# Root-mean-square norms: the inverse root by logarithm and exponential on the scalar engine, in place of an addition and a reciprocal on the vector engine around a root

## The chip, the cores and the metric

One core of one Trainium2 chip runs a whole two-block network in a single launch. The metric is the device time of that launch in microseconds (us). Five engines work side by side, each through its own list of instructions in order, and meet only at semaphores: TensorE (PE), VectorE (DVE), ScalarE (ACT), GpSimd (POOL) and SyncE (SP, which here only issues transfers).

## The reference: what is computed

A first block (adaptive norm, a mixer of four gated-delta-rule heads and four retention heads, a SwiGLU layer) and a second block (adaptive norm, windowed attention, a state-space scan and grid attention side by side, a merge, a convolutional feed-forward layer, a final norm), on 1024 latent tokens and 256 context tokens of 1024 features, all in fp32. What the change touches are the inverse roots in its norms:

```python
def rms_norm(x, g):
    y = xf * lax.rsqrt(jnp.mean(xf * xf, axis=-1, keepdims=True) + NORM_EPS)
def head_group_norm(t, g):
    return (t - mu) * lax.rsqrt(var + NORM_EPS) * g.astype(jnp.float32)
def l2_normalize(t):
    return t * lax.rsqrt(jnp.sum(t * t, axis=-1, keepdims=True) + NORM_EPS)
```

They are taken of the block's inputs (over 1024 features), of eight q and k heads of the delta rule (over 128), of its four outputs and of four retention outputs (over 128), of the state-space output (over 1024), of the q and k heads of grid attention (over 64), and of the residual stream (four times, over 1024).

## The kernel before, in words

The program is a row of stages, each with one function per engine (`gp_pe`, `gp_act`, `gp_dve`, `gp_pool` and so on). The order of each engine's instructions is the order in which these functions write them; there is no scheduler. Tiles are features (128 partitions) by tokens (up to 512 columns), and `LAT` is the two latent ranges of 512 tokens, `ALL` those and the context's 256. A `Ring` hands out buffers in turn; who takes one waits until the last user of that buffer has given it back. PSUM is eight banks of 128 x 512, mostly one ring, so a bank that is given back late can hold up PE.

Nearly every norm has one pattern. ACT squares the tile (`sq`), PE multiplies the squares by a matrix of ones, which leaves in a bank the sum over features, repeated over all partitions. Then DVE reads the bank and forms mean + epsilon in SBUF (`tensor_scalar`) and gives the bank back, ACT takes the square root in place (`AF.Sqrt`), and DVE inverts it in place (`reciprocal`). Only then the tile is multiplied by it, on DVE or on POOL.

The places, with the tiles' names in the profile:

- First stage (`a_*`, class `Rms`): `rstd`, three ranges. The three means and the three reciprocals stand between DVE's nine small steps of the modulation product `ad1` (`row` copies and `mod` additions), at the places that the tables `DUE` and `INV` name.
- Projection stage of the delta rule (`gp_*`): a first `softplus` for the decays (`tmp`), then twelve blocks m of q, k and v in the order k4 to k7, q0 to q3, v8 to v11. For a block PE multiplies three (or two) column ranges of h by w_in (`hT,wslot`), ACT copies them out (`raw`) and scales the first tap of a 5-tap convolution (`acc<-raw,par`), DVE adds the other four taps (`acc<-raw,par,acc`), ACT applies SiLU (`kT<-acc` or `qT<-acc`) and squares (`raw<-kT`), and PE sums (`raw,cst`). The inverse roots of a block (`rst`) come in DVE's list ahead of the taps of the next block, and POOL multiplies (`kT<-kT,rst`). PE's sums of block m-1 stand between the second and the last column range of block m. From the fifth block on ACT also copies the products of k by k out of the banks (`Wd`, `ktok`, `sq<-bank`).
- Gates of the delta rule and of retention (class `Gate`): `rgate`, four heads of two ranges each, while PE multiplies h by the gate's weights, and DVE also reduces tiles of the modulation matrix (`at1a`), with one small product of PE behind each.
- Projection of grid attention (class `AttGroup`, groups at20 and at21, `proj_*`): seven items of k and q, and in step j PE multiplies item j, sums the squares of item j-1, and rotates item j-2 (`at20qa`). `at20qc` holds the inverse root. For q DVE also multiplies by 1/8. Windowed attention (at10, at11) has the same functions without a norm.
- The residual stream's norms (class `SumSq`, tile `rcs`, 128 x 8) and the start of the second block (`fn_*`), and the state-space output (`ssr`).

ACT's functions lie in table sets, and an instruction ACT_TABLE_LOAD brings in another set. Before, none is written by hand; each stands ahead of the first activation that needs it.

Of the kernel before, what the change touches and what calls it, by code (L numbers as in the profile page):

```python
# [8 lines left out]
EPS = 1e-6  # L9
# [3 lines left out]
def const_tables():  # L13
# [19 lines left out]
        ("offB", ((i // 32) < (j // 32)).astype(f)),  # L33
    ]
# [62 lines left out]
def build(nc, io, out):  # L97
# [81 lines left out]
    class Eng:  # L179
# [124 lines left out]
    ident, ones = C("ident"), C("ones")  # L304
    hs = [slice(x * 128, (x + 1) * 128) for x in range(4)]
# [141 lines left out]
    class Rms:  # L447
# [48 lines left out]
        def mean_dve(self, e, n0, n):  # L496
            r = self.rstd[:, n0:n0 + n]
            e.wait_ge(*self.st.pe.after(self.nm, "sum", n0, self.nk - 1))
            e.tensor_scalar(r, self.banks[self.nm, n0][:, 0:n], self.inv, EPS, OP.mult, OP.add).then_inc(self.st.dve(self.nm, "ms", n0), 1)
            self.banks.give((self.nm, n0), self.st.dve.now())  # L500

        def inverse_dve(self, e, n0, n):
            r = self.rstd[:, n0:n0 + n]
            e.wait_ge(*self.st.act.after(self.nm, "rt", n0))
            e.reciprocal(r, r).then_inc(self.st.dve(self.nm, "rs", n0), 1)

        def dve(self, e):
            for n0, n in self.rngs:
                self.mean_dve(e, n0, n)
            for n0, n in self.rngs:  # L510
                self.inverse_dve(e, n0, n)
# [29 lines left out]
    def softplus(st, nm, x, y, tmp):  # L541
# [58 lines left out]
    DUE, INV = {0: 0, 2: 1, 5: 2}, {5: 0, 6: 1, 7: 2}  # L600
    nm1 = NormMod(n1, "h", xav, h1, ALL, [1, 0, 0], ad1.mv, 1, 0, "norm_mix_g", rstd, gs1, lambda n0: n1.dve.after("x", "rs", n0))
# [24 lines left out]
    def a_act(e):  # L626
# [5 lines left out]
        rms1.roots(e)  # L632
# [358 lines left out]
    def gp_act(e):  # L991
# [77 lines left out]
    def gp_dve(e):  # L1069
# [11 lines left out]
        def norm(m):  # L1081
            dst, rng = gp_dst(m)
            rst = rsts.take("rst", m)
            for ev in rsts.freed("rst", m):
                e.wait_ge(*ev)
# [3171 lines left out]
```

## Time and profile before

| what | value |
|---|---|
| three timed runs | 4667.87, 4677.79 and 4679.56 us, median 4677.79 |
| profiled execution, first to last instruction (span) | 4674.6 us |
| time of the profiled execution apart from its span | not given; the span is 3.2 us under the median of the runs |
| PE busy | 91% of the span |
| DVE busy | 51% |
| ACT busy | 33% |
| POOL busy | 19% |
| DVE, ACT and PE instructions | 3800, 2988 and 18566 |

The table is of averages over stages that differ: in the long matrix products PE has no gap, in others it waits for a chain through ACT and DVE. What an instruction less is worth shows only at the waits of the stage in which it stands. The rows for that are in the section below.

### The profile page before, as it was taken

To read this page: it belongs to the slowest core of one execution; us is meant where nothing else is said; L and a number is where in the kernel's file an instruction comes from. 1 tells how busy PE (TensorE), PEld (TensorE's weight loads), DVE (VectorE), ACT (ScalarE), POOL (GpSimd) and SP (SyncE) were. 2 spreads that over 40 slices of the span, in tenths; PEclk is the share of its full clock that TensorE was granted. 3 is DMA by queue.
4 is the path that set the end of the run, shared out by engine and by line. 5 is a ranking of instruction groups with operands and counts; after the bars stand their busy time and mean duration, and the time that the engine had idled before them with its cause. 6 is when DMAs were issued, how large, how long until landed. Compare 5 with 4: busy or idle time off the path is not lost.

```text
span 4674.6 us, 46418 instructions
## 1 busy us (share of the span) xinstructions
PE 4273.7 (91%) x18566; PEld 3110.9 (67%) x18566; DVE 2382.1 (51%) x3800; ACT 1548.5 (33%) x2988; POOL 905.8 (19%) x695
## 2 busy tenths in 40 slices
PE   7896789999999999997979999899888998999997
PEld 3455754767788888655557866565665677888886
DVE  2768864162556663336262327574657744333334
ACT  3465641122211111333233215352544633222222
POOL 2112224131344441007061000001000021000001
PEclk9898899999999999897979999999999999999999
DMA  5112243112333342211111210111000031111111
GB/s 194 41 61 86 73 133 107 34 52 81 86 113 113 113 115 59 88 58 62 39 61 49 82 44 19 37 57 56 17 23 19 19 117 37 54 45 54 43 39 63
DMA packets 257800, 308.90 MB, mean 66 GB/s; under 512 B 19072, under 2 KB 209936, under 8 KB 256304
## 3 DMA queue, kind: packets, MB, share of 16 engines
q1 hardware_dynamic: 238096, 227.15, 15.8%
q0 software_dynamic: 17408, 75.64, 5.2%
q8 instruction: 146, 2.39, 0.2%
q10 hardware_dynamic: 2080, 3.15, 0.2%
q14 instruction: 70, 0.57, 0.0%
HBM read 271.61 MB, written 34.28 MB: 65 GB/s over the span
## 4 chain that ended last, share of the span: by engine, by line
PE 61%; DVE 10%; ACT 5%; issue 1%; POOL 1%; DMA 0%; POOLq 0%; DVEq 0%; ACTq 0%
PE bank L193 60%; PE bank L196 2%; DVE Mx L205 1%; ACT Mx L202 1%; ACT at21P L202 1%; ACT at20P L202 1%; POOL sq L205 1%; DVE at20sm L223 1%; DVE at21sm L223 1%; DVE x L211 0%; DVE wfl L205 0%; DVE at21Pl L205 0%; DVE at11sm L223 0%; DVE at20Pl L205 0%; DVE at10sm L223 0%
## 5 line engine op out<-in xcount | busy, mean ns | idle before, releaser
L193 PE MATMUL bank<-h,wslot 128*128 128x512 f32 (+2 forms) x1616 | 686.4, 563 | 13.7 <-ACT h L202 3.6
L193 PE MATMUL bank<-hT,wslot 128*128 128x512 f32 (+3 forms) x1136 | 462.7, 564 | 15.9 <-DVE hT L211 7.3
L193 PEld LDWEIGHTS bank<-h,wslot 128*128 128x128 f32 (+1 forms) x1616 | 291.3, 191 | 242.3 <-issue 224.9
L193 PEld LDWEIGHTS bank<-hT,wslot 128*128 128x128 f32 (+1 forms) x1136 | 212.2, 189 | 241.6 <-issue 235.3
L193 PE MATMUL bank<-ffn1h,wfh 128*128 128x512 f32 x704 | 279.9, 398 | 11.8 <-DVE ffn1l L211 10.9
L211 DVE SCALAR_TENSOR_TENSOR x<-bank,mod,x 128x512 f32<-128x512 f32 x224 | 164.3, 746 | 245.4 <-PE bank L193 245.0
L193 PE MATMUL bank<-ffn2h,wgh 128*128 128x512 f32 x704 | 276.3, 392 | 10.0 <-DVE ffn2l L211 9.5
L193 PE MATMUL bank<-ffn1l,wfh 128*128 128x512 f32 x704 | 275.1, 391 | 0.0
L193 PE MATMUL bank<-ffn2l,wgh 128*128 128x512 f32 x704 | 274.7, 390 | 0.0
L193 PE MATMUL bank<-ffn1h,wfl 128*128 128x512 f32 x704 | 274.6, 390 | 0.0
L193 PE MATMUL bank<-ffn2h,wgl 128*128 128x512 f32 x704 | 274.5, 390 | 0.0
L205 DVE TENSOR_TENSOR wfl<-wslot,wfh 128x1024 fp32r<-128x1024 f32 (+2 forms) x92 | 150.3, 1634 | 148.1 <-ACT wfh L202 148.1
L205 POOL TENSOR_TENSOR ffn2al<-ffn2ga,ffn2ah 128x512 fp32r<-128x512 f32 x44 | 57.7, 1312 | 654.9 <-ACT ffn2ah L202 654.9
L226 DVE TENSOR_REDUCE at2a<-ffn1t 128x128 f32<-128x1024 f32 x72 | 143.1, 1988 | 47.8 <-POOL ffn1t L205 47.8
L205 POOL TENSOR_TENSOR sq<-sq 128x512 f32<-128x512 f32 (+1 forms) x77 | 95.0, 1233 | 361.0 <-ACT sq L202 356.8
L193 PEld LDWEIGHTS bank<-ffn1h,wfh 128*128 128x128 f32 x704 | 132.5, 188 | 44.7 <-DVE ffn1l L211 10.6
L193 PEld LDWEIGHTS bank<-ffn2h,wgh 128*128 128x128 f32 x704 | 132.5, 188 | 43.5 <-DVE ffn2l L211 10.6
L211 DVE SCALAR_TENSOR_TENSOR ffn2ga<-ffn2gw,par,ffn2ga 128x1024 f32<-128x1024 f32 x44 | 56.5, 1285 | 199.4 <-ACT ffn2ga L202 198.6
L193 PEld LDWEIGHTS bank<-ffn1h,wfl 128*128 128x128 f32 x704 | 132.6, 188 | 28.0
L193 PEld LDWEIGHTS bank<-ffn2h,wgl 128*128 128x128 f32 x704 | 132.6, 188 | 27.7
L193 PEld LDWEIGHTS bank<-ffn2l,wgh 128*128 128x128 f32 x704 | 132.6, 188 | 26.8
L193 PEld LDWEIGHTS bank<-ffn1l,wfh 128*128 128x128 f32 x704 | 132.8, 189 | 25.5
(573 smaller groups left out, 9512.8 us busy)
## 6 DMA issues: line engine op xcount, KB each, us to landing
wslot<-in_w_in SPq DMA_DIRECT2D x40, 1024.0 KB, 5.7
ffn1t<-in_w_mod POOLq DMA_DIRECT2D x64, 512.0 KB, 4.8
wslot<-in_w_ffn_in SPq DMA_DIRECT2D x44, 512.0 KB, 5.3
Mx<-acsT SPq DMA_DIRECT2D x32, 512.0 KB, 4.9
at1w<-in_ada_w POOLq DMA_DIRECT2D x24, 512.0 KB, 4.7
wslot<-in_ffn_w_gate SPq DMA_DIRECT2D x22, 512.0 KB, 4.0
wslot<-in_ffn_w_up SPq DMA_DIRECT2D x22, 512.0 KB, 5.3
wslot<-in_w_ffn_out SPq DMA_DIRECT2D x20, 512.0 KB, 5.4
```

The lines of the kernel that those rows point to most:

```text
L193: return Counted() if counting[0] else self.q.matmul(o, l, r, start=start, stop=stop)
L196: return Counted() if counting[0] else self.q.transpose(o, i, ident)
L202: return Counted() if counting[0] else self.q.activation(o, i, f, **k)
L205: return Counted() if counting[0] else self.q.tensor_tensor(o, a, b, op)
L211: return Counted() if counting[0] else self.q.scalar_tensor_tensor(o, a, s, b, op0, op1)
L223: return Counted() if counting[0] else self.q.reduce_max(o, a, AX.X)
L226: return Counted() if counting[0] else self.q.reduce_sum(o, a, AX.X)
```

## The change

Every such pattern but those of softmax is rewritten: 1/sqrt(v) is formed as exp(-0.5 ln v). ACT reads the sum from the bank itself (`AF.Ln`, with the 1/n as its scale and epsilon as its bias, a 128 x 1 pointer into three new constant columns), gives the bank back, and applies `AF.Exp` with scale -0.5 in place. DVE's `tensor_scalar` and `reciprocal` are gone. In the q blocks, where the factor 1/8 or 1/sqrt(128) belongs to the root, it goes into scale and epsilon (64 or 128 times each), so DVE's multiplication by 1/8 goes too. Whoever used the inverse root now waits for ACT. Table loads are written by hand: `ln_exp_table` brings the set that has both functions, and `exp_table` brings the exponential's own set at the end of each attention projection. `softplus`, which takes an exponential and then a logarithm, starts with the first of these.

```diff
+        ("eps", np.broadcast_to(np.array([EPS, 64 * EPS, 128 * EPS], f), (128, 3))),
...
+        def ln_exp_table(self):
+            if not counting[0]:
+                self.q.preload_act_table_set("natural_log_exp_and_others")
+
+        def exp_table(self):
+            if not counting[0]:
+                self.q.preload_act_table(AF.Exp)
...
-        def roots(self, e):
-            for n0, n in self.rngs:
-                e.wait_ge(*self.st.dve.after(self.nm, "ms", n0))
-                r = self.rstd[:, n0:n0 + n]
-                e.activation(r, r, AF.Sqrt).then_inc(self.st.act(self.nm, "rt", n0), 1)
+        def root(self, e, n0, n):
+            r = self.rstd[:, n0:n0 + n]
+            e.wait_ge(*self.st.pe.after(self.nm, "sum", n0, self.nk - 1))
+            e.activation(r, self.banks[self.nm, n0][:, 0:n], AF.Ln, scale=self.inv, bias=eps(1)).then_inc(self.st.act(self.nm, "ln", n0), 1)
+            self.banks.give((self.nm, n0), self.st.act.now())
+            e.wait_ge(*self.st.act.now())
+            e.activation(r, r, AF.Exp, scale=-0.5).then_inc(self.st.act(self.nm, "rs", n0), 1)
...
         def act(e):
+            e.ln_exp_table()
             e.wait_ge(*d.after(nm, "abs"))
             e.activation(ex, ex, AF.Exp, scale=-1.0).then_inc(a(nm, "exp"), 1)
...
     def a_dve(e):
         consts(e)
         for g in range(9):
-            if g in DUE:
-                rms1.mean_dve(e, *ALL[DUE[g]])
             ad1.dve(e, g)
-            if g in INV:
-                rms1.inverse_dve(e, *ALL[INV[g]])
...
         def norm(m):
-            rst = rsts["rst", m]
-            for n0, n in gp_dst(m)[1]:
-                e.wait_ge(*gp.dve.after("ss", m, n0))
-                e.activation(rst[:, n0:n0 + n], rst[:, n0:n0 + n], AF.Sqrt, scale=1.0 / QS ** 2 if m < 4 else 1.0).then_inc(gp.act("rt", m, n0), 1)
+            dst, rng = gp_dst(m)
+            rst = rsts.take("rst", m)
+            for ev in rsts.freed("rst", m):
+                e.wait_ge(*ev)
+            x = 128 if m < 4 else 1
+            e.ln_exp_table()
+            for n0, n in rng:
+                e.wait_ge(*gp.pe.after("norm", m, n0))
+                e.activation(rst[:, n0:n0 + n], bk_p["norm", m, n0][:, 0:n], AF.Ln, scale=float(x), bias=eps(x)).then_inc(gp.act("ln", m, n0), 1)
+                bk_p.give(("norm", m, n0), gp.act.now())
+            for n0, n in rng:
+                e.wait_ge(*gp.act.after("ln", m, n0))
+                e.activation(rst[:, n0:n0 + n], rst[:, n0:n0 + n], AF.Exp, scale=-0.5).then_inc(gp.act("rs", m, n0), 1)
...
-            for n0, n in rng:
-                e.wait_ge(*gp.pe.after("norm", m, n0))
-                e.tensor_scalar(rst[:, n0:n0 + n], bk_p["norm", m, n0][:, 0:n], EPS, None, OP.add).then_inc(gp.dve("ss", m, n0), 1)
-                bk_p.give(("norm", m, n0), gp.dve.now())
-            for n0, n in rng:
-                e.wait_ge(*gp.act.after("rt", m, n0))
-                e.reciprocal(rst[:, n0:n0 + n], rst[:, n0:n0 + n]).then_inc(gp.dve("rs", m, n0), 1)
...
                 if tn:
                     r = self.rsr[tn][:, 0:tn[3]]
-                    e.wait_ge(*st.dve.after("ms", *tn))
-                    e.activation(r, r, AF.Sqrt).then_inc(st.act("rt", *tn), 1)
+                    isq = tn[0] == "q"
+                    e.wait_ge(*st.pe.after("nm", *tn))
+                    e.activation(r, bk["nm", *tn][:, 0:tn[3]], AF.Ln, scale=1.0 if isq else 1.0 / 64, bias=eps(64 if isq else 1)).then_inc(st.act("ln", *tn), 1)
+                    bk.give(("nm", *tn), st.act.now())
+                    e.wait_ge(*st.act.now())
+                    e.activation(r, r, AF.Exp, scale=-0.5).then_inc(st.act("rs", *tn), 1)
...
             for gr in self.groups:
                 barrier(e, *gr.before)
                 gr.proj_act(e)
+                e.exp_table()
                 barrier(e, gr.sj)
                 gr.act(e)
```

`Gate`, `SumSq`, `fn_*` and the state-space output are changed in the same way.

Where the lists move, first on ACT, at the delta rule's `softplus` (`tmp`, `negA`, `bet`) and the copies `raw` of block k4 behind it. Before:

```order
L202 ACTIVATE ab<-bank 128x160
L202 ACT_TABLE_LOAD
L202 ACTIVATE tmp<-tmp 128x80
L202 ACT_TABLE_LOAD
L202 ACTIVATE tmp<-tmp 128x80
L202 ACT_TABLE_LOAD
L202 ACTIVATE negA<-par 128x80
L202 ACT_TABLE_LOAD
L202 ACTIVATE bet<-ab 128x80
L202 ACTIVATE raw<-bank 128x256
```

and of the change, at the same place:

```order
L203 ACTIVATE ab<-bank 128x160
L207 ACT_TABLE_LOAD
L203 ACTIVATE tmp<-tmp 128x80 x2
L203 ACTIVATE negA<-par 128x80
L203 ACT_TABLE_LOAD
L203 ACTIVATE bet<-ab 128x80
L203 ACTIVATE raw<-bank 128x256
```

Two of four table loads are gone there. The other two `softplus` calls change in the same way, and over the whole program ACT's list goes from 72 loads to 67.

Second, DVE's list in the projection stage, from the taps of k4 to those of k5 (the part for `rst` is that of the norm of k4). Before:

```order
L208 TENSOR_SCALAR nbet<-bet 128x80
L211 SCALAR_TENSOR_TENSOR acc<-raw,par,acc 128x1284 x4
L208 TENSOR_SCALAR rst<-bank 128x256
L208 TENSOR_SCALAR rst<-bank 128x512 x2
L217 RECIPROCAL rst<-rst 128x256
L217 RECIPROCAL rst<-rst 128x512 x2
```

and of the change:

```order
L217 TENSOR_SCALAR nbet<-bet 128x80
L220 SCALAR_TENSOR_TENSOR acc<-raw,par,acc 128x1284 x16
L223 COPY Gc<-bank 128x10x4 x2
L214 TENSOR_TENSOR kdf<-bank,Gc 128x80
L214 TENSOR_TENSOR bG<-bG,nbet 128x80
```

The norm of each block is gone from between the taps of two blocks, so that the taps of four blocks follow one another. The taps of the next block no longer have a norm of the last one ahead of them.

Third, ACT's list for the norm of k4, which stands ahead of the last `raw` copy and the first tap of k5. Before:

```order
L202 ACTIVATE raw<-bank 128x256
L202 ACTIVATE raw<-bank 128x512
L202 ACT_TABLE_LOAD
L202 ACTIVATE rst<-rst 128x256
L202 ACTIVATE rst<-rst 128x512 x2
L202 ACTIVATE raw<-bank 128x512
L202 ACTIVATE acc<-raw,par 128x1284
```

and of the change:

```order
L203 ACTIVATE raw<-bank 128x256
L203 ACTIVATE raw<-bank 128x512
L207 ACT_TABLE_LOAD
L203 ACTIVATE rst<-bank,cst 128x256
L203 ACTIVATE rst<-bank,cst 128x512 x2
L203 ACTIVATE rst<-rst 128x256
L203 ACTIVATE rst<-rst 128x512 x2
L203 ACTIVATE raw<-bank 128x512
L203 ACTIVATE acc<-raw,par 128x1284
```

One activation for each range is added there, and the number of loads is the same. PE's and POOL's lists do not change.

## Rows read from the trace of the kernel before

**Rows 1.** The page's first part: busy time of each engine.

```profile
PE 4273.7 (91%) x18566; PEld 3110.9 (67%) x18566; DVE 2382.1 (51%) x3800; ACT 1548.5 (33%) x2988; POOL 905.8 (19%) x695
```

**Rows 2.** Windows, all engines: the projection stage, and twenty us within it.

```profile
105.00:375.00 270.00, 226.70 (x677) 118.80 (x675) 192.18 (x184) 138.31 (x229) 36.30 (x27) 0.92 0.15 47
285.00:305.00 20.00, 19.73 (x62) 11.22 (x63) 10.51 (x6) 17.62 (x37) 3.79 (x3) 0.91 0.30 93
```

**Rows 3.** Groups by line and form: count, busy us, mean ns, idle before.

```profile
L217 DVE RECIPROCAL rst<-rst 128x512 f32<-128x512 f32 x16 | 52.3, 3309 | 14.2 <-ACT rst L202 14.0
L217 DVE RECIPROCAL at20qc<-at20qc 128x512 f32<-128x512 f32 x6 | 20.1, 3349 | 0.1
...
L202 ACT ACT_TABLE_LOAD x72 | 92.4, 1283 | 32.5 <-DMA par<-in_par 8.2 <-DVE gsc L211 5.3 <-PE bank L193 4.2
L202 ACT ACTIVATE at20P<-bank,at20sm 128x512 f32<-128x512 f32 x64 | 43.4, 683 | 14.3 <-DVE at20sm L208 14.3
```

**Rows 4.** Timeline of DVE, end of the first stage: start, us.

```profile
63.04 3.34 DVE L217 RECIPROCAL rstd<-rstd 128x512 f32<-128x512 f32 x1
66.30 0.10 DVE L205 TENSOR_TENSOR mod<-bank,par 128x4 f32<-128x4 f32 x1
```

**Rows 5.** Timeline of ACT, softplus of the delta rule.

```profile
110.13 1.28 ACT L202 ACT_TABLE_LOAD   x1
111.42 0.27 ACT L202 ACTIVATE tmp<-tmp 128x80 f32<-128x80 f32 x1
...
114.76 1.34 ACT L202 ACTIVATE raw<-bank 128x256 f32<-128x256 f32 x3
```

**Rows 6.** PE's waits from 104 to 375 us: in total, times, longest.

```profile
PE bank L193 <- ACT raw L202: 18.8, 8, 7.1
PE bank L196 <- ACT acc L202: 3.7, 1, 3.7
PE bank L196 <- DVE ktok L214: 3.3, 1, 3.3
PE bank L196 <- ACT kT L202: 2.3, 1, 2.3
```

**Rows 7.** Timeline of PE, projection stage: start, us, and in brackets idle before.

```profile
125.76 4.63 PE L193 MATMUL bank<-raw,cst 128*128 128x256 f32 x6 [7.05 <-ACT raw L202]
...
211.55 3.75 PE L193 MATMUL bank<-raw,cst 128*128 128x512 f32 x4 [3.85 <-ACT raw L202]
...
285.27 3.48 PE L193 MATMUL bank<-raw,cst 128*128 128x512 f32 x4 [2.94 <-ACT raw L202]
...
312.69 8.73 PE L193 MATMUL bank<-hT,wslot 128*128 128x512 f32 x16
...
352.73 7.03 PE L193 MATMUL bank<-hT,wslot 128*128 128x512 f32 x16
```

**Rows 8.** Timelines of DVE, ACT and POOL, blocks k4 and k6.

```profile
117.53 6.33 DVE L211 SCALAR_TENSOR_TENSOR acc<-raw,par,acc 128x1284 f32<-128x1284 f32 x4 [2.44 <-ACT acc L202]
160.17 7.12 DVE L211 SCALAR_TENSOR_TENSOR acc<-raw,par,acc 128x1284 f32<-128x1284 f32 x4
...
157.99 0.60 ACT L202 ACTIVATE raw<-bank 128x512 f32<-128x512 f32 x1 [4.90 <-PE bank L193]
...
160.34 2.42 POOL L205 TENSOR_TENSOR kT<-kT,rst 128x512 f32<-128x512 f32 x1 [1.94 <-DVE rst L217]
```

**Rows 9.** PE's waits from 600 to 740 us: gate and retention projection.

```profile
PE bank L193 <- ACT rr L202: 2.1, 1, 2.1
PE bank L193 <- DVE mod L205: 1.9, 2, 0.9
...
PE bank L193 <- DVE at1a L226: 1.4, 1, 1.4
```

**Rows 10.** PE's waits from 3197 to 3290 us: grid attention's projection.

```profile
PE bank L193 <- DVE at20qa L211: 2.4, 3, 1.4
```

**Rows 11.** Timeline of ACT, start of grid attention.

```profile
3277.56 1.28 ACT L202 ACT_TABLE_LOAD   x1 [4.13 <-DVE at20sm L208]
```

More of the change, by code:

```diff
@@ L494, in pool @@
                     sqr.give((self.nm, n0, k - 1), self.st.pool.now())
[L496 to L511, printed above, removed]
     class NormMod:
@@ L631, in a_act @@
         rms1.squares(e, [x.after("in") for x in xa_in])
-        rms1.roots(e)
+        e.ln_exp_table()
+        for n0, n in ALL:
+            rms1.root(e, n0, n)
         nm1.act(e)
@@ L1114, in gp_dve @@
         for i, m, rngs in QKV:
[L1115 to L1117 removed]
+            if i > 8:
                 v_tokens(m - 1)
@@ L1599, in root @@
             def root(x):
+                rst = self.rsts.take("r", x)
+                for ev in self.rsts.freed("r", x):
+                    e.wait_ge(*ev)
+                e.ln_exp_table()
                 for n0, n in LAT:
-                    r = self.rsts["r", x][:, n0:n0 + n]
-                    e.wait_ge(*st.dve.after("ms", x, n0))
-                    e.activation(r, r, AF.Sqrt).then_inc(st.act("rt", x, n0), 1)
+                    e.wait_ge(*st.pe.after("norm", x, n0))
+                    e.activation(rst[:, n0:n0 + n], self.bk["norm", x, n0][:, 0:n], AF.Ln, scale=1.0 / 128, bias=eps(1)).then_inc(st.act("ln", x, n0), 1)
+                    self.bk.give(("norm", x, n0), st.act.now())
+                for n0, n in LAT:
+                    e.wait_ge(*st.act.after("ln", x, n0))
+                    e.activation(rst[:, n0:n0 + n], rst[:, n0:n0 + n], AF.Exp, scale=-0.5).then_inc(st.act("rs", x, n0), 1)
             root(0)
@@ L1646, in norm @@
             def norm(x):
-                rst = self.rsts.take("r", x)
-                for ev in self.rsts.freed("r", x):
-                    e.wait_ge(*ev)
-                for n0, n in LAT:
-                    e.wait_ge(*st.pe.after("norm", x, n0))
-                    e.tensor_scalar(rst[:, n0:n0 + n], self.bk["norm", x, n0][:, 0:n], 1.0 / 128, EPS, OP.mult, OP.add).then_inc(st.dve("ms", x, n0), 1)
-                    self.bk.give(("norm", x, n0), st.dve.now())
+                rst = self.rsts["r", x]
                 for n0, n in LAT:
                     r, a = rst[:, n0:n0 + n], self.y[:, self.at(x, n0, n)]
-                    e.wait_ge(*st.act.after("rt", x, n0))
-                    e.reciprocal(r, r).then_inc(st.dve("rs", x, n0), 1)
-                    e.wait_ge(*st.dve.now())
+                    e.wait_ge(*st.act.after("rs", x, n0))
                     e.stt(a, a, P(self.gname), r, OP.mult, OP.mult).then_inc(st.dve("n", x, n0), 1)
@@ L2622, in fn_act, with root @@
         barrier(e, ffn1.st, at2.st)
-        e.wait_ge(*d.after("v1"))
-        e.activation(rn1[:, :], rn1[:, :], AF.Sqrt).then_inc(a("s1"), 1)
+        e.wait_ge(*ffn1.ss.st.pe.end())
+        def root(r, s, key):
+            e.activation(r, s, AF.Ln, scale=1.0 / D, bias=eps(1)).then_inc(a("ln", key), 1)
+            e.wait_ge(*a.now())
+            e.activation(r, r, AF.Exp, scale=-0.5).then_inc(a(key), 1)
+        e.ln_exp_table()
+        root(rn1[:, :], bank[6][:, 0:16].rearrange("p (c w) -> p c w", w=2)[:, :, 0], "r1")
         e.wait_ge(*cx_in.after(1))
@@ L2633, in fn_act @@
         squares(range(2))
-        e.wait_ge(*d.after("v2"))
-        e.activation(rn2[:, :], rn2[:, :], AF.Sqrt).then_inc(a("s2"), 1)
+        e.wait_ge(*d.after("q2"))
+        root(rn2[:, :], rn2[:, :], "r2")
         squares(range(2, 8))
-        e.wait_ge(*d.after("vc"))
-        e.activation(rcc, rcc, AF.Sqrt).then_inc(a("sc"), 1)
+        e.wait_ge(*fn.pe.after("cs"))
+        root(rcc, bank[4][:, 0:2], "rc")
         for n0, n in ALL[1:] + ALL[:1]:
@@ L3315, in sz_act @@
             if (kind, m) == ("g", 2):
-                rms_y.roots(e)
+                e.ln_exp_table()
+                for n0, n in LAT:
+                    rms_y.root(e, n0, n)
         for t in range(18, 24):
@@ L3621, in proj_act @@
             st, bk = self.sj, self.bk
+            if not self.win:
+                e.ln_exp_table()
             for j in range(len(self.items) + 2):
```

72 lines of the change are left out of this document (18 added, 54 removed).

## The prediction

> **What bounds the kernel now.** I read the page's busy times first: PE is busy 91% of the span, DVE 51%, ACT 33% [rows 1]. So PE's own instructions set most of the time, and this change touches none of them. All that it can win is time in which PE stands still for a chain through ACT and DVE, and the work taken from DVE is no measure of it. That work is large: a reciprocal of a 128x512 tile takes 3.3 us [rows 3], and forty-eight of that size go, some 160 us. The share of those that PE waits for must be read stage by stage, so next came the windows: in the projection stage of the delta rule PE works 226.7 of 270 us at a mean clock of 0.92, and DVE 192.2 [rows 2]. That is the stage where DVE could be late. Then PE's waits of each stage that holds a norm: 28.1 us in the projection stage [rows 6], 5.4 in the gate and behind it [rows 9], 2.4 in each of two grid-attention projections [rows 10]. In the retention gate and around the state-space output PE has no wait on these tiles, and I count nothing there though eight and two reciprocals go. The timelines then showed, for each wait, whether a reciprocal or a table load lies on the chain that ends it.
>
> **What the pieces cost.** A mean and a reciprocal leave DVE, a root on ACT becomes two activations. The trace has no Ln and no Exp on these tiles. The nearest row is an activation that reads a 128x512 bank with a pointer as bias, 683 ns [rows 3], and I take that for both at most. A chain over DVE, ACT and DVE, 3.3 us of it the reciprocal, becomes at most 1.4 us on ACT alone. A table load takes 1.28 us, and the next activation starts 0.01 us after its end [rows 5]. The list has five fewer of them.
>
> A page speaks otherwise: by the Trainium skill, "ScalarE: Activation LUTs", section "What ACT_TABLE_LOAD costs", a switch costs about 2.66 us, the load and a drain of 1.38. By that page each load off the path would be worth twice what the rows say. The trace shows no such drain, so the sum goes by 1.28, and the other is a rival below.
>
> **The change part by part.**
>
> *First stage.* DVE's last reciprocal runs from 63.04 us, and the last `mod` addition, on which all of the norm's multiplications wait, has to stand behind it until 66.30 [rows 4]. PE's part of that addition is done some 0.5 us after the reciprocal starts (an estimate from the length of PE's four small products there). Gain 2.8 us, at least 0 and at most 3.3. The banks of the first two sums are now given back by ACT behind its squares, a little later for PE in mid-stage, ahead of weights that it waits for anyway: nothing.
>
> *Softplus of the delta rule.* Two loads go from a chain that has no slack: the `raw` copies start right behind it at 114.76 [rows 5], DVE's taps behind those, and PE waits 7.05 us for the squares at the end [rows 7]. Gain 2.5.
>
> *Blocks k4 to v8.* Here the chain per block is: PE's last range, ACT's `raw` copy and first tap, DVE's four taps, SiLU, square, PE's sum. The reciprocals of the last block lie ahead of the taps. In k6 the taps start at 160.17, only 0.2 us after ACT's first tap (its `raw` copy starts at 157.99), so the reciprocal there costs almost nothing by itself; but they take 7.12 us where those of k4 took 6.33, while POOL's late multiplication takes 2.42 us beside them [rows 8]. With the root done on ACT ahead of PE's last range POOL is through before the taps start, and 0.8 us a block comes back. From q0 on the reciprocals also delay the start of the taps. Going through PE's waits:
> - eight waits for ACT's `raw`, 18.8 us [rows 6]. 7.05 is treated above. 3.85 before q0's sums [rows 7]: the taps start earlier by what the reciprocal hangs over (about 0.9, an estimate) and run 0.8 shorter, gain 1.7. 2.94 before q3's [rows 7]: the taps wait for a reciprocal behind ACT's delayed root, all of it goes, 2.9. Of the other five (4.9 together) the three shortest go, about 1.6; the two that wait for ACT and PE themselves stay.
> - one wait for DVE's k copies, which stand behind a reciprocal, 3.3 [rows 6]: gain 2.8.
> - one for v8's SiLU, 3.7 [rows 6], behind the last reciprocals and slow taps: all of it.
> - one for ACT's `kT`, 2.3 [rows 6]: the 0.8 of the taps.
>
> Together 13.5. After the 3.7 us wait sixteen products took 8.73 us where they take 7.03 in full clock [rows 7]; without the wait I count these 1.7 as well. Bounds for the stage, softplus in it: 17.7 as summed; at least 8 if ACT becomes the pace (below); at most 25, if the slower clock behind the other waits comes back too. Work of DVE that follows block v10 does not get shorter, but it waits for PE's last range there, so PE's gain is handed on.
>
> *What ACT pays there.* Each block has up to 1.4 us more on ACT. In k6 ACT stood idle 4.9 us before its last `raw` copy [rows 8], which hides it. From q2 to v8 it does not: ACT is busy 17.6 us of 20 from 285 to 305 [rows 2]. I have let this delay the taps of q3 and v8 by 1.3 us each; the waits above are long enough to hold it.
>
> *Delta-rule gate.* PE waits 1.4 us for `at1a` and 1.9 for `mod` [rows 9], both of which DVE reaches late because of two reciprocals a head. Gain 3.3; at least 0. The wait for the reload of h at its start stays. *Softplus of retention:* two loads, 2.6 us, go from the chain to the first `rr` copy, for which PE waits 2.1 [rows 9]: gain 2.1.
>
> *Grid attention.* In the last three steps DVE's list (two rotations, two splits, reciprocal, 1/8, product) is longer than PE's step, and PE waits 2.4 us in three pieces for `at20qa` [rows 10]; without the 3.3 us of a reciprocal alone it is shorter. Gain 2.4. At its end the exponential's table is loaded at 3277.56, after the wait for the scores' maximum [rows 11]; the hand-written load comes ahead of that barrier. Gain 1.3. Both stages, at20 and at21, are alike: 7.4. Windowed attention's first group has the same load on the same place: 1.3. Its second group gets a load that it did not have, in a gap of ACT: nothing, at worst 1.3.
>
> *Norms of the residual stream.* They are 8 columns wide; three short instructions on two engines become two on one. I take nothing for the four.
>
> **Sum.** 2.8 + 2.5 + 13.5 + 1.7 + 3.3 + 2.1 + 7.4 + 1.3 = 34.6 us off a span of 4674.6, which stands 3.2 us under the median of the three runs shown. Median after: 4677.8 - 34.6 = 4643.2 us. If all lower bounds held it would be about 16 us (4662), with all upper ones some 44 (4634).
>
> **The rivals.**
> - *ACT becomes the pace.* What speaks for it: the 17.6 of 20 us, and a new order in which ACT stands in its own list waiting for PE's sums, with the next `raw` copy queued behind. Against it: in the K blocks those sums are PE's next instructions, and ACT has 4.9 us. It decides once the added work exceeds the idle time ahead of the `raw` copy; that is so from q2 on. The three long waits there (2.9 + 3.3 + 3.7) and the clock's 1.7 would be half kept, and the gates' 3.3 not won: 34.6 - 9 - 3 gives about 22 less, 4655.
> - *Little of it arrives.* Later chains wait for something else anyway, such as transfers or POOL, and eat the gain at the next stage's barrier. Only the attention stages (8.7) and a few us remain, under what a measurement of this kernel tells from no change (0.3%, 14 us): 4669.
> - *Loads cost twice.* Seven loads leave the path (two and two in softplus, three before attention). Did each cost as much again in a drain behind it, 9 us would come on top: 4634. The 0.01 us between load and activation speaks against it, and so the page named above with it.
> - *More clock returns.* PE's clock is 0.92 in the projection stage. If closing the waits lifted it to 1.0 throughout, some 8 us more than I count, and with the upper bounds elsewhere: 4628.
> - *Slower.* The one mechanism is ACT's list order: at each of the sixteen norms of delta-rule blocks and gates and retention gate, ACT now stands at PE's sums (3.5 us for q3's [rows 7]) and adds 1.4. If PE in turn waited for what is queued behind, 4.9 us each time, 78 would come against the 35 won: 4721. This needs ACT's gap ahead of the next copy to be under 4.9 us; in k6 it is 4.9 [rows 8], with PE's sums in it already.
> - *The change does not do what it says:* that would be loads put in again around each pair. The list shows none (67 against 72), so it has no chance of its own.
>
> **How the numbers follow.** The sum as it stands (4635 to 4652): 0.56. ACT as pace (to 4663): 0.17. Little arrives: 0.09. Loads twice: 0.05. More clock: 0.09. Slower: 0.04. The likeliest is the sum, 4643. The range takes the first, most of ACT's case, the loads and most of the clock's: 4626 to 4663. Faster by over 0.3% (under 4663.8): 0.56 + 0.17 + 0.05 + 0.09 = 0.87. Slower by as much: 0.04. Within: 0.09.
>
> **What the changed profile would show.** No reciprocal left on `rst`, `rgate`, `rstd`, `ssr`, `at20qc`; 67 loads at 1.28 us; Ln on a 128x512 bank near 0.68 us, Exp no longer. The last `mod` of the first stage near 63.5 us. The taps of k5 to k7 at 6.3 us, not 7.1. PE's waits of the projection stage down from 28.1 to about 12, without those for `ktok` and `acc`, and v10's end some 20 us earlier. In the gate no wait of PE for `mod` or `at1a`. In grid attention no wait for `at20qa`, and at20P right behind its maximum. The prediction is wrong if PE's waits for ACT's `raw` in the q blocks stay as long as they were (ACT is the pace), if PE's clock falls below 0.92 there, or if a stage behind, above all the delta rule's scan from 375 us on, starts earlier and ends where it ended.

## The result and the profile after

The changed kernel takes 4622.9 us (median of 4 runs, 4619.3 to 4628.1), the kernel before beside it 4672.8 (4 runs, 4661.7 to 4679.6). The ratio is 0.9895, with a 95% interval of 0.9881 to 0.9908: some 50 us less, where I had forecast 34.6 and a time of 4643. The time lies below my range, whose low end was 4626.

The page of the changed kernel answers to [rows 1] (busy us, share of the span, instructions):

```profile
span 4620.0 us, 46359 instructions
PE 4249.3 (92%) x18566; PEld 3097.0 (67%) x18566; DVE 2177.3 (47%) x3670; ACT 1573.8 (34%) x3044; POOL 900.7 (19%) x695
```

PE has the same 18566 products as before and needs 24.4 us less for them (4273.7 in [rows 1]). No edit touches a product, so that part is the clock, but for some 0.3 us with each wait (see the forced waits below). PE's time outside them fell from 400.9 to 370.7 us, by 30.2; I had forecast 32.9 of waits (34.6 without the clock's 1.7). So in this pair of traces the waits came nearly as forecast, and the clock gave far more. A second trace of before, below, has 4269.2 us of products and 392.2 outside them, so both differences carry an uncertainty of 4 to 9 us that one pair doesn't show; what holds is read stage by stage.

Since both kernels have the same products in the same order, a stage can be cut at the same product in both. Windows cut so, first of before (projection stage of the delta rule, its gate, windowed attention, grid attention), then of after; the columns are us, then busy time of PE, PEld, DVE, ACT and POOL, the granted clock as a share of its upper level (1.00 is 2.4 GHz, the lower level 1.2 GHz is 0.50), the DMA share and GB/s:

```profile
105.16:376.13 270.97, 226.54 (x677) 118.82 (x676) 192.18 (x184) 139.44 (x230) 36.30 (x27) 0.92 0.15 46
620.19:725.35 105.16, 89.67 (x271) 44.46 (x270) 69.74 (x84) 36.83 (x66) 30.01 (x23) 0.97 0.43 138
2722.48:3197.48 475.00, 439.62 (x2001) 291.59 (x2001) 267.00 (x797) 194.25 (x565) 38.64 (x31) 0.96 0.14 44
3197.48:3757.90 560.42, 499.81 (x2325) 336.54 (x2326) 376.51 (x801) 276.73 (x663) 15.24 (x12) 0.95 0.07 22
```

```profile
102.68:351.30 248.62, 219.18 (x678) 115.64 (x676) 118.05 (x144) 146.70 (x248) 29.33 (x27) 0.94 0.16 51
593.51:694.72 101.21, 88.89 (x270) 44.63 (x269) 46.71 (x68) 38.64 (x72) 30.00 (x23) 0.97 0.45 145
2689.41:3156.74 467.33, 432.73 (x2001) 286.77 (x2001) 266.47 (x797) 195.76 (x567) 38.62 (x31) 0.98 0.14 45
3156.74:3704.94 548.20, 494.59 (x2326) 333.33 (x2326) 320.48 (x764) 284.16 (x676) 15.18 (x12) 0.96 0.07 23
```

The stages gave 22.4, 4.0, 7.7 and 12.2 us, where I had 17.7, 3.3, 1.3 and 7.4. Of that, 7.4, 0.8, 6.9 and 5.2 us are PE's busy time, of which I had counted 1.7, in the first. The third is the striking one: hardly a wait changed there, and it is 7.7 us shorter.

The waits of PE in the projection stage of after answer to [rows 6] (total us, number, longest):

```profile
PE bank L194 <- ACT raw L203: 10.1, 4, 4.6
PE bank L197 <- ACT kT L203: 1.4, 1, 1.4
PE bank L197 <- ACT acc L203: 1.3, 2, 1.1
```

Together 12.8 us where [rows 6] had 28.1; I had said about 12. The wait for `ktok` is gone. Groups of instructions on ACT (us busy, mean ns):

```profile
L203 ACT ACTIVATE rst<-bank,cst 128x512 f32<-128x512 f32 x16 | 10.3, 684 | 1.4 <-PE bank L194 1.4
L203 ACT ACTIVATE rst<-rst 128x512 f32<-128x512 f32 x16 | 9.2, 628 | 0.0
```

The logarithm takes 684 ns and the exponential 628, against the 3309 of a reciprocal [rows 3]. DVE's taps in k5 to k7 take 6.33 us again:

```profile
154.38 6.33 DVE L220 SCALAR_TENSOR_TENSOR acc<-raw,par,acc 128x1284 f32<-128x1284 f32 x4 [13.40 <-ACT acc L203]
```

### The profile page after: what moved, and what is told of

The parts are those of the page before. It is cut to its first block, busy times and chain, and to the rows that moved or that the text cites. A ratio compares the mean times of both kernels' runs of the same rounds, so it can differ in the third digit from the quotient of the medians.

```text
span 4620.0 us, 46359 instructions
## 1 busy us (share of the span) xinstructions
PE 4249.3 (92%) x18566; PEld 3097.0 (67%) x18566; DVE 2177.3 (47%) x3670; ACT 1573.8 (34%) x3044; POOL 900.7 (19%) x695
## 4 chain that ended last, share of the span: by engine, by line
PE 63%; DVE 9%; ACT 5%; POOL 2%; issue 1%; DMA 0%; POOLq 0%; DVEq 0%; ACTq 0%
PE bank L194 61%; PE bank L197 2%; DVE Mx L214 1%; ACT at21P L203 1%; ACT at20P L203 1%; ACT Mx L203 1%; POOL sq L214 1%; DVE at21sm L232 1%; DVE at20sm L232 1%; DVE x L220 1%; DVE wfl L214 0%; DVE at20Pl L214 0%; DVE at21Pl L214 0%; DVE at11sm L232 0%; DVE at10sm L232 0%
## 5 line engine op out<-in xcount | busy, mean ns | idle before, releaser
L194 PE MATMUL bank<-ffn1h,wfh 128*128 128x512 f32 x704 | 279.8, 397 | 11.8 <-DVE ffn1l L220 10.9
```

Source lines behind the costliest of these rows:

```text
L194: return Counted() if counting[0] else self.q.matmul(o, l, r, start=start, stop=stop)
```

## Experiments

Two theories stand against each other for the missing 15 to 20 us. **A**: a closed wait gives TensorE's clock back as well, and I priced that far too low. **B**: which stretches run at the lower clock differs from one execution to the next, and the two traces happened to lie on either side. The windows of all thirteen traces are cut at the same products of PE. Ratios below are to the kernel before, run on the same chip.

**The same two kernels again.** No edit.

> The kernel before once more, for the spread of TensorE's clock from one execution to the next. In its first trace PE stood 424.8 us at the lower of its two levels, 34.1 of them in windowed attention (2722 to 3197 us), 59.0 in grid attention (3197 to 3757), 42.8 in the projection stage (105 to 375); in the trace of the changed kernel these were 366.2, 17.0, 44.4 and 27.6. Theory A (the clock was given back because of the change): the numbers of this second trace lie within 5 us of the first in every stage, and the ratio is 1.000 within 0.001. Theory B (where a low stretch falls is chance, and the two traces happened to lie on either side): stages move by 10 us and more from one execution to the next, the total by 20 or more, and the runs spread by over 10 us.

Measured: 4667.9 us (12 runs, 4663.2 to 4680.7) beside 4670.0 (20 runs), ratio 1.000 [0.9989, 1.0014]. The windowed and grid stages of this second trace of before:

```profile
2717.99:3186.29 468.30, 432.80 (x2000) 286.61 (x2001) 267.83 (x797) 193.99 (x565) 38.67 (x31) 0.98 0.14 45
3186.29:3743.87 557.58, 496.31 (x2325) 333.30 (x2326) 376.69 (x801) 276.59 (x663) 15.23 (x12) 0.96 0.07 22
```

Windowed attention takes 468.3 us here and 475.0 in the first trace, with nothing changed: a difference like the 7.7 us comes without any change, as B has it. The projection stage has 270.9 us both times and 0.92; there it is not chance. Neither theory came whole: A allowed 5 us a stage, B wanted 10 and more. And thirty-two runs put the kernel before at 4668 to 4670, not at the 4677.8 that I started from.

> The changed kernel once more. Theory A: ratio 0.989 to 0.990 again, some 366 us at the low level, 17 in windowed attention. Theory B: the ratio drifts to about 0.992 (the 34.6 us of closed waits and 3 to 5 us of clock behind them), the low level to some 385 us, windowed attention to some 25.

Measured: 4624.2 us (5 runs), ratio 0.9895 [0.9879, 0.9910]; projection stage 249.6, windowed 467.4, grid 548.1 us, about 354 us at the low clock in all (from the mean granted clock; in the same way 423 and 417 us in the two traces of before, 364 in the first of the changed kernel). The ratio does not drift towards 0.992, so chance explains a stage, and not the whole.

**Parts of the change alone.** The first has the norms of the delta rule's projection and the table load ahead of both softplus; in it `Rms`, `Gate`, `SumSq` and `AttGroup` are as before:

```
+            e.ln_exp_table()                    # in softplus's act
+                e.activation(rst, bk_p["norm", m, n0][:, 0:n], AF.Ln, scale=float(x), bias=eps(x))
+                e.activation(rst, rst, AF.Exp, scale=-0.5)
-                e.reciprocal(rst[:, n0:n0 + n], rst[:, n0:n0 + n])
```

> The norms of the delta rule's projection stage and the two softplus alone; first stage, gates, residual norms, state-space output and attention as before. My prediction's terms: 2.5 + 13.5 + 1.7 + 2.1 = 19.8 us, ratio 0.9958. By the trace of the changed kernel the stage gave 22.4 and the retention softplus 0: ratio 0.9952. If the clock comes back further on merely because everything starts earlier (Theory B), windowed attention changes by several us here though nothing in it is changed; by Theory A the stages behind 725 us keep their length within 2 us.

Measured: 4651.3 us, ratio 0.9956 [0.9940, 0.9972]. The forecast for this part was 0.9958. The projection stage has all of its gain, and windowed attention takes 468.6 with nothing changed in it:

```profile
106.42:355.97 249.55, 220.15 (x677) 116.42 (x676) 118.07 (x144) 146.92 (x248) 29.38 (x27) 0.95 0.16 50
2704.25:3172.87 468.62, 433.06 (x2001) 286.98 (x2001) 267.17 (x797) 194.00 (x565) 38.65 (x31) 0.97 0.14 45
```

The second has `AttGroup`'s roots and the `exp_table` loads alone:

```
+                    e.activation(r, bk["nm", *tn][:, 0:tn[3]], AF.Ln, scale=1.0 if isq else 1.0 / 64, bias=eps(64 if isq else 1))
+                    e.activation(r, r, AF.Exp, scale=-0.5)
-                    e.reciprocal(r, r)
+                e.exp_table()
```

> The roots of grid attention by logarithm and exponential and the exponential's table loaded ahead of the barrier in all four attention groups; all else as before. My prediction's terms: 7.4 + 1.3 = 8.7 us, ratio 0.9981. The trace of the changed kernel has 19.9 us less from 2722 to 3757 us, of which only 7.7 are idle time of PE: Theory A says that the same comes here (ratio 0.9957, windowed attention 7.6 us shorter), Theory B that windowed attention comes to within 3 us of before and the ratio to 0.997 to 0.9985.

Measured: 4658.2 us, ratio 0.9967 [0.9954, 0.9980]. Grid attention takes 547.9 us as in the changed kernel, and the ratio's 11.8 us by the medians are more than the 8.7 of my sum. Windowed attention takes 470.6, between the 468.3 and 475.0 of before. The gain of grid attention is real: 557.6 to 560.6 us in the four traces whose norms there are as before, 546.2 to 550.9 in the eight with the change. Their means differ by 11.0 us, 7.5 of it idle time of PE and 3.5 busy time. Of windowed attention one trace can't say it.

The third has the rest: first stage, gates, residual norms, state-space output (`Rms.root`, `Gate`'s and `SumSq`'s roots as in the diff of the change, nothing else).

> First stage, both gates, the residual norms and the state-space output by logarithm and exponential; the delta rule's projection norms, the softplus loads and attention as before. My prediction's terms: 2.8 + 3.3 = 6.1 us, ratio 0.9987. The two traces of the changed kernel against those of before have 2.0 us less in the first stage, 4.0 in the gate and 2.2 in the state-space scan (2012 to 2545), where I had forecast nothing: if that scan's part belongs to the changed norms around it, it comes here too (533 to 530.5); if it comes of the softplus loads or of chance, it does not.

Measured: 4662.0 us, ratio 0.9979 [0.9969, 0.9989]. My terms for this part were 6.1 us, the medians give 6.4. The gate has 3.2 us of its own (102.0), the scan (2012 to 2545) takes 533.4 us, no less than before: the 2.2 us that I saw there don't come from these norms, and over all the traces that stage scatters by more. Two rows:

```profile
103.19:369.88 266.69, 226.49 (x677) 119.27 (x676) 193.01 (x184) 135.43 (x227) 36.45 (x27) 0.92 0.15 47
2708.65:3187.02 478.37, 442.99 (x2000) 293.82 (x2001) 266.93 (x797) 194.29 (x565) 38.65 (x31) 0.95 0.14 44
```

Windowed attention takes 478.4 us here, 11 more than in the changed kernel and 10 more than in the second trace of before, and none of its instructions differs from before. The projection stage is 4.3 us shorter although its norms are as before: the first stage leaves the table of logarithm and exponential loaded, and three loads of the softplus's chain go with it. So this gain can be had from either side, and the parts' gains overlap by it. Here PE's busy time stayed (226.5 us) though 4.2 us of waits went. The three parts' ratios add up to 0.0098 less, the whole has 0.0105, which the intervals don't tell apart.

**The reciprocals back on DVE,** in the changed kernel, in the projection stage and in grid attention:

```
-                e.activation(rst, rst, AF.Exp, scale=-0.5).then_inc(gp.act("rs", m, n0), 1)
+                e.activation(rst, rst, AF.Exp, scale=0.5).then_inc(gp.act("rs", m, n0), 1)
+                e.reciprocal(rst[:, n0:n0 + n], rst[:, n0:n0 + n])      # DVE, ahead of the next taps
```

> The changed kernel, but in the delta rule's projection stage and in grid attention ACT's exponential gives the root and DVE inverts it where it did before: no square root and no addition, the same table loads as in the changed kernel, twenty-seven large reciprocals back on DVE. If the reciprocals' time in DVE's list is what PE waited for (my prediction), the projection stage goes from 249 us to about 262 to 266, with the waits for ktok and the last acc back, and each grid attention stage gets 2.4 us of waits for at20qa back. If it was the hand-over from DVE to ACT and back and the square root's tables, most of the gain stays: stage under 255 us, grid attention within 1 us of the changed kernel. PE's busy time of the projection stage tells what the clock does: by my reading of the first traces it rises again by 5 to 7 us with 15 us of idle time.

Measured: 4659.7 us (8 runs), ratio 0.9972 [0.9960, 0.9984]. PE's waits of the projection stage, and the stage:

```profile
PE bank L194 <- ACT raw L203: 24.4, 8, 7.0
PE bank L197 <- ACT acc L203: 4.9, 1, 4.9
PE bank L197 <- DVE ktok L223: 4.1, 1, 4.1
PE bank L197 <- ACT kT L203: 2.4, 1, 2.4
```

```profile
102.71:379.83 277.12, 224.97 (x678) 119.33 (x676) 181.48 (x164) 147.40 (x248) 37.43 (x27) 0.93 0.15 46
```

(By the list 28 reciprocals of 128x512 and six of 128x256 are back.) DVE and POOL in block k6:

```profile
156.38 7.12 DVE L220 SCALAR_TENSOR_TENSOR acc<-raw,par,acc 128x1284 f32<-128x1284 f32 x4
156.54 2.42 POOL L214 TENSOR_TENSOR kT<-kT,rst 128x512 f32<-128x512 f32 x1 [1.92 <-DVE rst L226]
```

The stage is longer than ever before, 277 us, 11 over the top of what I expected. Perhaps the reciprocals come later because they stand behind two activations in place of one root; that is not shown. The waits for `ktok` and the last `acc` are back, and so are the taps' 7.12 us with POOL's 2.42 us multiplication beside them. So the reciprocals in DVE's list are enough to undo all of the stage's gain, with the square root's tables and DVE's additions still gone, and the rival that put the gain there (under 255 us) is out. What came back is two things at once, the reciprocals' time and the hand-over from ACT to DVE; this run doesn't divide the 28.5 us between them, and so doesn't prove that the time alone was what PE waited for before. Busy time rose by 5.8 us with 22.7 us of waits, the direction A wants, at a lower price than in the other traces. In grid attention (553.2 us, 5.0 more than the changed kernel) only 0.9 us of the 2.4 us wait for `at20qa` came back in at20 and in at21; the rest of that wait went with DVE's additions and the multiplication by 1/8, which stay gone here.

**No early load of the exponential's table.**

```
-                e.exp_table()
```

> The changed kernel without the hand-written load of the exponential's table ahead of the attention stages, so that it is loaded behind the wait for the scores' maximum again. By the rows (load 1.28 us, next activation 0.01 us behind it) PE's idle time grows by 1.3 us in each of three groups (the first windowed one, both grid ones), 3.9 together, 4 to 6 with the clock; if a load cost 2.66 us, by 2.7 us each, 8 together.

Measured: 4628.7 us (4 runs), ratio 0.9911 [0.9893, 0.9929], which does not tell it from the changed kernel (I expected 4 to 6 us more, and the medians have 4.5 to 6.4 more). Grid attention takes 547.9 us, as with the load. Only the first windowed group loads late; ACT there without the hand-written load, then with it:

```profile
2773.59 1.28 ACT L203 ACT_TABLE_LOAD   x1 [2.50 <-DVE at10sm L217]
2775.09 0.46 ACT L203 ACTIVATE at10P<-bank,at10sm 128x256 f32<-128x256 f32 x1
```

```profile
2766.25 1.28 ACT L211 ACT_TABLE_LOAD   x1
2768.94 0.46 ACT L203 ACTIVATE at10P<-bank,at10sm 128x256 f32<-128x256 f32 x1
```

PE's wait for `at10P` there is 4.0 us long with the load ahead and 4.9 without, in all thirteen traces; its idle time in the stage went from 34.6 to 35.2 us. The stage takes 478.0 us here, though. Over all thirteen traces it took 468.3, 468.6, 475.0, 478.0 and 478.4 us where the load comes late, and 467.3 to 470.7 in the eight where it comes early. With so few traces that can be chance, but it is not shown that the early load has no part in it: the mean difference is 5.1 us, of which 1.0 is idle time. In the grid groups the table that the norms' logarithm loaded also serves the softmax: the 1.3 us I gave to the hand-written load came from the Ln and Exp pair, and three of the four hand-written loads do nothing. Where a load is on the path it costs 1.3 us or less, not 2.66. Nor does a drain show where ACT had not been waiting: in the delta rule's projection of the changed kernel an activation ends at 122.57 us, the load runs from 122.58 to 123.86, and the logarithm starts at 123.88.

**What a wait costs.** In most of the second feed-forward stage PE has no gap and full clock. There I made 40 waits:

```
+                if self.holds(t):                                   # PE, 8 down products of 5 groups
+                    e.wait_ge(*st.pool.after("hold", t))
+                    e.wait_ge(*st.pe.after("mm", self.tiles[i - 1], 512))   # POOL
+                    e.memset(self.hold[:, :], 0.0)                  # 2, 3, 5, 3, 5 times
```

> The changed kernel with waits made on purpose in the second feed-forward stage, where PE is otherwise busy without a gap at full clock: ahead of each of the 8 products of five groups, PE waits for POOL, which waits for PE's last product and then fills a scratch tile 2, 3, 5, 3 and 5 times (about 0.65 us each by the longer fills in the trace): 8 waits of some 1.4 us, 16 of 2.1, 16 of 3.4. The stage took 726.4 us in every trace. Theory A (a closed wait also gives clock back): PE's busy time in the groups with 2.1 and 3.4 us waits grows as well, by about 0.45 us for each us of wait, as in the projection stage (15.0 us of idle time and 6.7 of busy time went together) and in grid attention (7.3 and 3.2); little behind the 1.4 us ones. Rival: the clock does not answer to waits of this length, and the busy time that fell came by chance or from elsewhere: the stage grows by the waits alone, busy time the same within 1 us a group.

Each of these products is a run of 24 matmuls. Measured: 4812.8 us (2 runs), ratio 1.030. The same matmuls in the changed kernel (the eight products and what follows them directly), then the five groups, which have waits of 15.3, 21.2, 33.1, 21.2 and 33.1 us:

```profile
3880.67:3940.80 60.13, 60.13 (x267) 49.76 (x266) 19.70 (x18) 20.21 (x24) 7.87 (x6) 1.00 0.17 47
```

```profile
3957.20:4037.30 80.10, 64.76 (x266) 50.75 (x266) 22.68 (x28) 10.08 (x14) 12.12 (x17) 0.96 0.19 53
4107.80:4201.20 93.40, 72.16 (x266) 55.99 (x265) 22.68 (x28) 10.11 (x14) 17.57 (x25) 0.89 0.16 45
4271.70:4382.90 111.20, 78.14 (x266) 60.49 (x265) 22.68 (x28) 10.11 (x14) 28.46 (x41) 0.83 0.13 38
4453.40:4546.40 93.00, 71.76 (x266) 55.83 (x265) 22.68 (x28) 10.08 (x14) 17.57 (x25) 0.89 0.16 46
4616.90:4727.60 110.70, 77.64 (x266) 60.25 (x265) 22.68 (x28) 10.06 (x14) 28.46 (x41) 0.83 0.11 31
```

The same 266 matmuls take 4.6, 12.0, 18.0, 11.6 and 17.5 us more busy time: 0.30, 0.57, 0.54, 0.55 and 0.53 us for each us of wait. The first wait of a group is longer than the others (4.2 to 6.4 us, POOL starts late); the seven others last 1.6, 2.3 or 3.8. Not all of it is clock. With a 1.6 us wait before it a product takes 5.75 us of busy time at a clock of 1.00, where it took 5.44 without: 0.31 us comes with a wait as such. Less 0.31 for each of the eight waits, the groups with the longer waits have 0.43 to 0.47 us of clock for each us, close to the 0.45 that I expected. Of the first group 2.1 us are left, and they stand behind its 4.2 us wait. How it looks behind a wait of 3.81 us: products at 0.43 us spacing, and at 0.23 again from 4652.77 on.

```profile
4642.53 0.39 PE L194 MATMUL bank<-ffn2ah,wgl 128*128 128x512 f32 x1
4646.73 0.80 PE L194 MATMUL bank<-ffn2ah,wgh 128*128 128x512 f32 x1 [3.81 <-POOL hold L238]
4647.32 0.63 PE L194 MATMUL bank<-ffn2al,wgh 128*128 128x512 f32 x1
...
4652.01 0.63 PE L194 MATMUL bank<-ffn2ah,wgh 128*128 128x512 f32 x1
4652.44 0.49 PE L194 MATMUL bank<-ffn2al,wgh 128*128 128x512 f32 x1
4652.77 0.40 PE L194 MATMUL bank<-ffn2ah,wgl 128*128 128x512 f32 x1
```

In the trace each of the fourteen 3.8 us waits has such a stretch, and nine of the fourteen 2.3 us ones (five of seven in the second group, four of seven in the fourth); of the 1.6 us ones none. A was right in its price for waits of 2.3 us and more.

**A version that beats both.** Two pieces moved in the changed kernel: the delta rule's softplus, `negA` and `bet` behind the first block's squares (ACT) and taps (DVE), and one reduction of the modulation on DVE behind the retention softplus:

```
-        gsp_act(e)                               # ahead of the blocks; the same on DVE
+            if i == 0:
+                gsp_act(e)                       # behind block 0's squares; on DVE behind its taps
-                    if self.tiles:
+                    if self.tiles and (m, n0) != (3, 512):
                         self.tiles.dve(e, m * 2 + n0 // 512)
+        at1.dve(e, 7)                            # behind the four Dk in the retention projection
```

> The changed kernel with two pieces of work moved. (1) The delta rule's softplus, negA and bet go from ahead of the first block to behind its squares on ACT and behind its taps on DVE. PE waits 4.6 us for that block's squares, and the chain is 3.7 us shorter on ACT and 5.3 on DVE: 3.7 to 4.6 us less idle time, and by the clock 1 to 3 more. If the softplus then delays the second block, part comes back there. (2) The retention softplus goes ahead of one reduction of the modulation on DVE. In the changed kernel its 128x8 addition took 2.58 us and ended 0.05 us after a 1.91 us multiplication on POOL (1.22 us before, the same 0.04 us behind POOL's end). If POOL's work blocks it, the addition takes 0.2 us now and PE's wait of 2.1 us for rr goes; if the 2.58 us have another reason, they stay. Together 5 to 9 us below the changed kernel: 4616 to 4620, ratio 0.988.

> The kernel with both pieces moved, once more beside the changed kernel. Its waits fell by 3.4 us in the projection stage and 2.5 in the gate and the retention projection, its profiled execution came out no shorter. If that was the spread of the clock, it is 6 to 9 us below the changed kernel by the medians again; if the clock takes the gain back, within 3 us.

> The changed kernel, for the comparison with the one above: some 4623 us, ratio 0.9895.

Measured: 4615.1 us (5 runs), ratio 0.9881 [0.9865, 0.9898], and again 4612.7 (4 runs), 0.9876 [0.9862, 0.9891]; the changed kernel beside the second 4622.4 (4 runs), 0.9896 [0.9880, 0.9913]. So it is 9.7 us below the changed kernel beside it, and each of its four runs (4611.0 to 4616.8) is below each of that kernel's four (4619.9 to 4624.9), though the intervals of the ratios touch; the first five runs, which had none of that kernel's beside them, are 7 to 9 us below its three medians. The projection stage takes 242.9 us (after: 248.6), with 3.4 us less idle time and 2.3 less busy time (3.1 to 3.3 less against the other two traces of the changed kernel). The retention softplus explains itself. DVE and POOL in before:

```profile
712.82 1.22 DVE L208 TENSOR_SCALAR rt<-rt 128x8 f32<-128x8 f32 x1 [1.55 <-ACT rt L202]
```

```profile
712.09 1.91 POOL L205 TENSOR_TENSOR at1w<-at1w,sc 128x1024 f32<-128x1024 f32 x1
```

DVE, POOL and, later, PE in after, and last DVE in the moved version:

```profile
680.86 2.58 DVE L217 TENSOR_SCALAR rt<-rt 128x8 f32<-128x8 f32 x1 [0.19 <-ACT rt L203]
```

```profile
680.54 0.93 POOL L241 DMA_DIRECT2D at1w<-in_ada_w  x1 [4.23 <-DVE mod L214]
681.48 1.91 POOL L214 TENSOR_TENSOR at1w<-at1w,sc 128x1024 f32<-128x1024 f32 x1
```

```profile
694.72 1.13 PE L194 MATMUL bank<-rr,cst 128*128 128x512 f32 x2 [2.12 <-ACT rr L203]
```

```profile
676.33 0.17 DVE L217 TENSOR_SCALAR rt<-rt 128x8 f32<-128x8 f32 x1 [1.05 <-ACT rt L203]
```

The addition of 128x8 numbers ended 0.04 us behind POOL's multiplication in before (714.04 and 714.00) and 0.05 in after (683.44 and 683.39), and takes 0.17 us where POOL is idle. In before this cost nothing, since a table load on ACT ran beside it (712.81 to 714.09) and the chain waited for that anyway. PE's wait for `rr` is gone in the moved version. By the Trainium skill, "SBUF — State Buffer", section "Who interferes with whom", a `tensor_scalar` of DVE that uses DVE's second ports as well and an instruction of POOL exclude each other for a whole instruction, and the one that was issued first goes first. The rows of before agree with it, if this addition is such a one. In after DVE's row begins 0.62 us ahead of POOL's multiplication, while POOL was still issuing a transfer (680.54 to 681.47), so the rule alone doesn't say why DVE had to wait for the multiplication's end; that is open.

## Why the prediction was wrong, step by step

- **The sum's start.** I took 4677.8, the median of three runs. The runs of before made since then, in four sets, have medians of 4667.9 to 4670.0. The forecast's 34.6 us from there would have been 4634: 9 us of the miss of 20. The range, 9 us lower, would have held the measured time; the gain would still have been too small, 34.6 us where the medians measured side by side differ by 45.8 to 50.0.
- **The clock's term, 1.7 us, is the step that failed.** "Without the wait I count these 1.7 as well" priced one wait of the projection stage and put the clock behind all others at nothing. Busy time fell by 7.4 us there (6.4 in the part alone) with 15.0 us of waits, and in grid attention by 3.5 with 7.5 us of waits, by the means of four and eight traces. The forced waits show the price for waits of 2.3 us and more, 0.53 to 0.57 us of busy time for each us of wait, 0.43 to 0.47 of it clock. Other changes of the waits fell outside it: 0.25 with the reciprocals back, none in the third part, 0.7 to 1.0 in the moved version. Of the rivals "more clock returns" came nearest, 4628, but not as it was put: the clock of that stage went from 0.92 to 0.94, not to 1.0, and more of it came in grid attention.
- **First stage, 2.8.** Right: the last `mod` addition is at 63.78 us, [rows 4] had 66.30; gain 2.5.
- **Blocks k4 to v8 and softplus, 13.5 + 2.5 of waits.** Right: PE's idle time went from 44.4 to 29.4 us, 15.0. The waits for `ktok` and `acc` and the taps' 7.12 us fell as said. "ACT becomes the pace" did not happen: the waits for `raw` fell from 18.8 to 10.1 us. Block v10's products end at 334.94 us, 24.8 earlier than in [rows 7]; I had said 20. The scan behind, which I had named as a sign of being wrong should it end where it ended, took 242.2 us (before 244.1) and kept the gain.
- **Gate, 3.3.** Right: 4.0, 3.2 in the part alone; no wait for `mod` or `at1a` is left.
- **Retention softplus, 2.1.** Wrong: 0. The two loads went, and DVE's addition, held until the end of POOL's multiplication, took what they had saved. PE still waits 2.1 us for `rr`.
- **Grid attention, 7.4.** The size of its waits was right (60.6 us of idle time before, 53.6 after: 7.0; 7.5 by the means), and no wait for `at20qa` is left. One cause was not right: the 1.3 us a stage came from the shared table, not from the hand-written load. The clock came on top.
- **Windowed attention, 1.3.** 0.8 us of idle time. The other 7 us are PE's busy time, which moves as much with nothing changed (467.3 to 478.4 us for the stage over the traces, idle time 34.2 to 35.6 in all of them). That it fell in this pair was luck at least in part; whether the early load makes the long executions rarer is open.
- **Loads cost twice.** Wrong: without the early load one wait grew by 0.9 us, far from 2.66, and no drain shows beside any load looked at.
- **Slips in the sums.** Half of the three long waits and of the clock's 1.7 is 5.8 us, not 9, so "ACT becomes the pace" comes to 4652, not 4655; the bounds as written add up to 17.5 and 42.4 us, not 16 and 44. None moves the forecast.
- **What stays open:** the effect of chance on the first pair of traces is read from thirteen traces and not controlled. The stages named give some 30 us of waits and 10 of busy time; of the 46 to 50 by the medians the rest is not placed. Windowed attention's 5 us could be part of it.

## What to carry to other kernels

Price a wait of TensorE of 2.3 us or more at about one and a half times its length, since in the forced waits here the clock fell behind most of them (single changes gave anything from the bare length to nearly twice), and take the kernel's time from more than three runs before a forecast of 1%. A reciprocal of a large fp32 tile on DVE (3.3 us) is worth replacing by logarithm and exponential on ACT (1.3 us together) where something on DVE's list behind it is waited for and ACT has the time; count that, not DVE's busy time. When a chain is shortened, look at what the other engines do at its new place.

## What the runs showed of the hardware

- Seven waits of 1.6 us left the clock at its upper level (2.4 GHz); nine of fourteen of 2.3 us, and all fourteen of 3.8 us, were followed by a stretch at the lower one (1.2 GHz). A wait of 1.6 us at full clock still cost 0.31 us of busy time.
- The same instructions with the same waits (windowed attention with the late load, idle time 35.2 to 35.6 us) took 468 to 478 us from one trace to another, by the clock alone.
- A 0.17 us instruction on DVE took 2.58 us, ending 0.05 us behind the end of a multiplication on POOL, in every trace where it stood at that place; in before 1.22 us, also ending with POOL's.
- A table load took 1.28 us on average, with 0.01 to 0.02 us to the activations on either side where they follow directly, and Exp after Ln needs none once both come from one table: that also served a softmax a barrier later.
